# Turning the expert tiles on VectorE in 32x32 blocks, in a two-block decoder kernel

## The reference, cut to what matters

```python
def peer_ffn(h, w_q, sub_keys, expert_u, expert_v):       # 8 heads, 128 x 128 = 16384 experts, top 16
    q = (xb @ w_q).reshape(PEER_BLOCK, PEER_HEADS, 2, PEER_HALF)
    s = jnp.einsum('thjd,hjkd->thjk', q, sub_keys).astype(jnp.float32)
    sv, si = lax.top_k(s, PEER_TOPK)
    cand = sv[:, :, 0, :, None] + sv[:, :, 1, None, :]
    cs, ci = lax.top_k(cand.reshape(PEER_BLOCK, PEER_HEADS, PEER_TOPK * PEER_TOPK), PEER_TOPK)
    ...
    eidx = i1 * PEER_N_KEYS + i2
    g = jax.nn.softmax(cs, axis=-1)
    act = jax.nn.gelu(jnp.einsum('td,thkd->thk', xb, expert_u[eidx]), approximate=False)
    return jnp.einsum('thk,thkd->td', (g * act).astype(v.dtype), expert_v[eidx])
```

## Time and profile before

| | us |
|---|---|
| median of 3 runs | 5112.97 |
| lowest, highest | 5112.11, 5113.0 |
| the profiled execution | 5112.5 |
| its span | 5110.8 |

### The profile page before, as it was taken

One profiled execution on the slowest core, in us unless ns is written; L12 is line 12 of the kernel. 1 busy time (PEld: TensorE's weight loads), 2 busy tenths in 40 slices (PEclk: granted clock), 3 DMA queues, 4 the chain that ended last, 5 costly groups with the idle time before them and its releaser, 6 DMA issues. The chain is left out here.

```text
span 5110.8 us, 60896 instructions
## 1 busy us (share of the span) xinstructions
PE 4680.5 (92%) x23260; PEld 3922.2 (77%) x23260; DVE 2321.4 (45%) x3698; ACT 1421.5 (28%) x1441; POOL 355.4 (7%) x213
## 2 busy tenths in 40 slices
PE   8998998998996879978887799899999999999997
PEld 6886667887885668867777687678888888888886
DVE  4323234324324543224666433356665764455554
ACT  3222432213212332223333212232223333222222
POOL 0000000000000000001111000000000000233331
PEclk9998999999997689978999899999999999999999
DMA  3232012232231022221111222223333444555553
GB/s 107 96 93 70 30 41 74 96 96 87 88 101 42 0 66 93 90 57 58 50 49 41 62 75 94 76 72 125 127 126 128 156 185 168 195 195 195 191 189 114
DMA packets 446288, 511.43 MB, mean 100 GB/s; under 512 B 22104, under 2 KB 394964, under 8 KB 445156
## 3 DMA queue, kind: packets, MB, share of 16 engines
q1 hardware_dynamic: 446180, 510.01, 29.9%
HBM read 440.74 MB, written 69.21 MB: 100 GB/s over the span
## 5 line engine op out<-in xcount | busy, mean ns | idle before, releaser
L78 DVE TENSOR_TENSOR w_lo<-w_raw,w_hi 128x2048 fp32r<-128x2048 f32 (+2 forms) x322 | 672.0, 2089 | 1291.4 <-ACT w_hi L72 1291.4
L72 ACT CAST w_hi<-w_raw 128x2048 fp32r<-128x2048 f32 (+2 forms) x322 | 555.5, 1729 | 1130.6 <-PE psum L2738 491.6
L95 PE MATMUL psum<-h_lo_ffn,w_hi 128*128 128x512 f32 x1280 | 498.2, 389 | 0.0
L96 PE MATMUL psum<-h_hi_ffn,w_lo 128*128 128x512 f32 x1280 | 498.2, 389 | 0.0
L94 PE MATMUL psum<-h_hi_ffn,w_hi 128*128 128x512 f32 x1280 | 498.2, 389 | 0.0
L94 PE MATMUL psum<-h_hi_peer,w_hi 128*128 128x512 f32 x1120 | 445.3, 398 | 3.1 <-DVE w_lo L78 1.9
L96 PE MATMUL psum<-h_hi_peer,w_lo 128*128 128x512 f32 x1120 | 437.3, 390 | 0.0
L95 PE MATMUL psum<-h_lo_peer,w_hi 128*128 128x512 f32 x1120 | 436.4, 390 | 0.0
L2738 PE MATMUL psum<-pr_act_hi,w_lo 128*128 128x512 f32 x1024 | 398.6, 389 | 0.0
L2736 PE MATMUL psum<-pr_act_hi,w_hi 128*128 128x512 f32 x1024 | 398.6, 389 | 0.0
L2737 PE MATMUL psum<-pr_act_lo,w_hi 128*128 128x512 f32 x1024 | 398.6, 389 | 0.0
(11 more groups left out here) (441 smaller groups left out, 8333.1 us busy)
## 6 DMA issues: line engine op xcount, KB each, us to landing
w_raw<-in_ffn_w_gate_up_dram SPq DMA_DIRECT2D x176, 512.0 KB, 4.2
w_raw<-in_peer_u_dram SPq DMA_DIRECT2D x128, 512.0 KB, 4.1
w_raw<-in_peer_v_dram SPq DMA_DIRECT2D x128, 512.0 KB, 4.3
w_raw<-in_w_in_dram SPq DMA_DIRECT2D x64, 512.0 KB, 4.4
peer_hidden<-pr_q SPq DMA_DIRECT2D x64, 512.0 KB, 2.6
peer_gates<-pr_staged SPq DMA_DIRECT2D x8, 4096.0 KB, 12.7
pr_back<-peer_hidden SPq DMA_DIRECT2D x64, 512.0 KB, 6.2
pr_gate<-peer_gates SPq DMA_DIRECT2D x64, 512.0 KB, 7.2
```

The costliest lines, as they stand in the source:

```text
L72: c.nc.scalar.copy(c.hi[:, slot, :cols], c.raw[:, slot, :cols]).then_inc(c.hi_ready, 1)
L78: c.nc.vector.tensor_tensor(c.lo[:, slot, :cols], c.raw[:, slot, :cols], c.hi[:, slot, :cols].bitcast(F32), ALU.subtract).then_inc(c.lo_re ...
L95: c.nc.tensor.matmul(out, w_hi, x_lo, start=False, stop=False)
L96: mm = c.nc.tensor.matmul(out, w_lo, x_hi, start=False, stop=(n == last))
```

## The change

- `turn` moves from TensorE to VectorE: one block transpose of the raw tile in place, each 32x32 block by itself. For that a U tile is loaded in another arrangement, in four DMAs of 32 partitions each with runs of 1 KB. After the turn, partition 32b + j holds features 256b + 32k + j in chunk k, an order of features that differs from that of h. So h is stored in DRAM after the first query tiles and loaded back in that order, chunk by chunk as the last query (now with the chunk as outer loop) frees them.
- hi and lo of a U tile are made from SBUF in two halves, `by_chunk` and `turned_part`.
- `hide` uses banks 0 and 1 or 2 and 3 in turn, and may start before the gelu of the unit ahead.
- Order in a spreading unit: VectorE builds the middle quads of unit x, turns tile n+1, builds the first quads of unit x+1, makes lo of n+1. ScalarE copies hi of n+1 first, then stages all quads.
- `second` of a quad is made by one tensor_tensor instead of four instructions.
- In the norms of width 512 (eight of them) the sum of a token lands in a [128, 4] tile, the root and the reciprocal work on that, and the factor is spread over the identity and summed by a second matmul with ones, which leaves it in PSUM.
- The top-8 steps raise one semaphore at their end instead of one an instruction.

```diff
@@ Norm.vector, Norm.tensor
+        if self.by_token:
+            nc.vector.tensor_scalar(self.col[:, :], self.ps[:, 0, 0:TC], 1.0 / D, EPS, ALU.mult, ALU.add
+                                    ).then_inc(self.steps, 1)
+            dve.wait_ge(self.rooted, run + 1)
+            nc.vector.reciprocal(self.col[:, :], self.col[:, :]).then_inc(self.steps, 1)
...
+            nc.vector.tensor_tensor(rstd[:, :].rearrange("p (t k) -> p t k", t=TC),
+                                    self.c.ident[:, :].unsqueeze(1).broadcast_to(tokens),
+                                    self.col[:, :].unsqueeze(2).broadcast_to(tokens), ALU.mult
+                                    ).then_inc(self.spread, 1)
...
+            for t in range(TC):
+                ins = mm(self.ps[:, 0, t:t + 1], self.sq[:, 0, t * P:(t + 1) * P], self.c.ones[:, 0:1], start=True,
+                         stop=True)
+            ins.then_inc(self.summed, 1)
+            pe.wait_ge(self.spread, self.run + 1)
+            mm(self.ps[:, 0, :], self.c.ones[:, :], self.rstd[:, :], start=True, stop=True).then_inc(self.widened, 1)
@@ SyncE
             def u_tile(use, j, n):
-                load_tile(c, sp, use, j, u_parts(c, j, u, n * 2))
+                sp.wait_ge(c.begun, 1)
+                sp.wait_ge(c.lo_ready, 2 * use + j + 1)
+                rows = u.rearrange("(q e) d -> e q d", e=BAND)
+                for b in range(P // BAND):
+                    dst = c.raw[b * BAND:(b + 1) * BAND, j, :].rearrange("p (q n) -> p q n", n=BAND * KD)
+                    src = rows[:, bass.ds(n * 8, 8), b * BAND * KD:(b + 1) * BAND * KD]
+                    sp.dma_start(dst, src).then_inc(c.tile_loaded[j], 16)
+            def store_h():
+                sp.wait_ge(pre.lo_done, (pre.run + 1) * KD)
+                for m in range(2):
+                    for k in range(KD):
+                        odd, r = k // 4, k % 4
+                        src = h[m][r * BAND:(r + 1) * BAND, odd:KD:2, :].bitcast(F32)
+                        sp.dma_start(h_rows[m, k].rearrange("(b j) t -> j b t", j=BAND), src).then_inc(h_stored, 16)
+            def reload_h():
+                sp.wait_ge(h_stored, ROWS_LOADED + 16 * 2 * KD)
+                for k in range(KD):
+                    sp.wait_ge(h_free, k + 1)
+                    for m in range(2):
+                        sp.dma_start(h[m][:, k, :].bitcast(F32), h_rows[m, k]
+                                     ).then_inc(h_back[k // 4], 16)
...
-            for n in range(3):
-                u_tile(uA + n // 2, n % 2, n)
+            u_tile(uA, 0, 0)
+            u_tile(uA, 1, 1)
+            reload_h()
+            u_tile(uA + 1, 0, 2)
@@ ScalarE
+            def copy_hi(j):
+                for a in range(2):
+                    ins = nc.scalar.copy(by_chunk(c.hi, j, a), turned_part(c, j, a))
+                ins.then_inc(c.hi_ready, 1)
...
                 for x in range(ROUND_UNITS):
                     before, between = quads_of(x)
+                    j = (x + 1) % 2
+                    act.wait_ge(turned, o * ROUND_UNITS + (SPREAD_AT + x + 2))
+                    copy_hi(j)
                     stage(o, before)
-                    act.wait_ge(turned, o * ROUND_UNITS + (SPREAD_AT + x + 2))
-                    act.wait_ge(c.tile_used, o * ROUND_UNITS + (2 * uA + SPREAD_AT + x + 2))
-                    nc.scalar.copy(c.hi[:, (x + 1) % 2, :], turn_ps).then_inc(c.hi_ready, 1)
                     stage(o, between)
@@ VectorE
+            def turn(n):
+                j = n % 2
+                dve.wait_ge(c.tile_loaded[j], 32 * uA + 64 * (n // 2) + 64)
+                dve.wait_ge(c.tile_used, 2 * uA + n + 1)
+                V.transpose(c.raw[:, j, :], c.raw[:, j, :]).then_inc(turned, 1)
...
+                    V.tensor_tensor(second[:, k % RING], c.iota[:, :].unsqueeze(1).broadcast_to(wide),
+                                    chosen[:, 1, toks].unsqueeze(2).broadcast_to(wide), ALU.is_equal)
...
             for n in range(CHOSEN_AT):
-                turned_lo(n)
+                turn(n + 1)
                 piece(EARLY + n)
+                turned_lo(n + 1)
...
+            build(0, quads_of(0)[0])
             for o in range(SPREAD_ROUNDS):
                 for x in range(ROUND_UNITS):
-                    before, between = quads_of(x)
-                    build(o, before)
-                    build(o, between)
-                    turned_lo(SPREAD_AT + o * ROUND_UNITS + x + 1)
+                    n = SPREAD_AT + o * ROUND_UNITS + x + 1
+                    build(o, quads_of(x)[1])
+                    turn(n)
+                    if x + 1 < ROUND_UNITS:
+                        build(o, quads_of(x + 1)[0])
+                    elif o + 1 < SPREAD_ROUNDS:
+                        build(o + 1, quads_of(0)[0])
+                    turned_lo(n)
@@ TensorE
-            pe.sem_inc(gelued, 1)
+            pe.sem_inc(gelued, 2)
...
+            hide(uA, 0, 0, h_is_back)
+            hide(uA, 1, 1)
+            with pe.Fori(1, CHOSEN_AT // 2) as i:
-                turn(uA + i, 1)
                 hide(uA + i, 0, i * 2)
-                turn(uA + i + 1, 0)
                 hide(uA + i, 1, i * 2 + 1)
...
                     spread_quads(o, before)
-                    turn(follow, (x + 1) % 2)
                     wait_tile(c, pe, use, x % 2)
```

More of the change, by code:

```diff
@@ L350, in tensor @@
         pe.wait_ge(self.steps, self.run * self.STEPS + 4)
[L351 to L354, removed]
+        mm = self.c.nc.tensor.matmul
+        if self.by_token:
+            for t in range(TC):
[4 more added lines that the diff above has]
+            mm(self.ps[:, 0, :], self.c.ones[:, :], self.rstd[:, :], start=True, stop=True).then_inc(self.widened, 1)
+        else:
+            for b, (lo, hi) in enumerate(self.banks):
+                ins = mm(self.ps[:, b, :], self.c.ones[:, :], self.sq[:, 0, lo:hi], start=True, stop=True)
+            ins.then_inc(self.summed, 1)
+            pe.sem_inc(self.spread, 1)
+            pe.sem_inc(self.widened, 1)
 def norm(c, tag, gain, h, src=None, width=T, out_f32=None):
@@ L2250, in quads_of, with groups_ended_in, peer @@
     return range(at, at + a), range(at + a, at + a + b)
-def peer(c, gain, w_q, sub_keys, u, v, h, hidden, gates):
+def groups_ended_in(x):
+    before, between = quads_of(x)
+    begin, end = before.start, between.stop
+    return [g for g in range(ROUND_GROUPS) if begin < (g + 1) * GROUP_QUADS <= end]
+def peer(c, gain, w_q, sub_keys, u, v, h, hidden, gates, h_rows):
     nc = c.nc
@@ L2347, in _ @@
                 sp.sem_inc(written[j], 16)
-            with sp.Fori(1, NH // 2) as i:
+            for i in range(1, NH // 2):
                 for j in range(2):
@@ L2655, in queries @@
                 n = i * 2 + j
+                last = isinstance(i, int) and i == NH // 2 - 1 and j == 1
                 if not (isinstance(i, int) and i == 0):
@@ L2658, in queries @@
                     pe.wait_ge(q_taken, n - 1)
+                if last:
+                    jobs = wide_jobs(c, h, j)
+                    for k in range(KD):
+                        for out, pair, _ in jobs:
+                            (w_hi, w_lo), (x_hi, x_lo) = pair(k)
+                            nc.tensor.matmul(out, w_hi, x_hi, start=k == 0, stop=False)
+                            nc.tensor.matmul(out, w_hi, x_lo, start=False, stop=False)
+                            mm = nc.tensor.matmul(out, w_lo, x_hi, start=False, stop=k == KD - 1)
+                        mm.then_inc(h_free, 1)
+                    pe.sem_inc(c.tile_used, 1)
+                elif not (isinstance(i, int) and i == 0):
                     w_hi, w_lo = w_tile(c, j, KD, 256)
@@ L2752, in _ @@
             scores(0, 0)
-            with pe.Fori(1, NH // 2) as i:
+            with pe.Fori(1, NH // 2 - 1) as i:
                 queries(i, 0)
```

167 lines of the change are left out of this document (93 added, 74 removed).

## The result

The changed kernel takes 5069.6 us (median of 12 runs, 5067.7 to 5096.5) against 5111.4 us (12 runs, 5110.6 to 5113.0): a ratio of 0.9938, 95% interval 0.992 to 0.9955. Its runs form two groups with nothing between them: seven at 5067.7 to 5069.9 and five at 5094.8 to 5096.5. The kernel before has one group. The profiled execution is one of the lower group: 5068.3 us, span 5066.6.

The account below looks back on a forecast made before the run. TensorE's list of work bounds the expert layer's long stages. Gains of 2 + 43.2 + 8.9 + 5 less losses of 1 + 38.7 + 1.5 make 17.9 us: 5112.5 to 5095 us, range 5040 to 5150.

Parts of the forecast that it names:

- The turn's price: VectorE's transpose of a 128x2048 tile takes 2.21 us; rival, a slow turn, 5192 us at 4.4 us, chance 0.12.
- the forecast's 2.65: Turn time in us on VectorE at which the whole gain is gone, at 44 us lost per microsecond above 2.21.
- First stage: Units 0 to 33 of the expert layer: 58.4 us from turns off TensorE, less 15.2 given back, 43.2 gained.
- the third kind just fits: First stage: VectorE's turn, lo and third-costliest piece take 10.67 us, within TensorE's 10.89 us a unit.
- the fifth kind: First stage: the fifth kind of VectorE piece is as short as the fourth, which fits easily at 8.35 us.
- Spreading: 24 units of the expert layer: three take 57.65 us against 52.81, so 38.7 us lost, plus 1.5 in the first.
- The stop of 7.4 us: Every third spreading unit: TensorE waits 7.4 us before its third quad on ScalarE's staging, plus 2.0 us of clock.
- The start and the last units: Expert layer's start: 2 us gained by the first hide, 1 lost to stores; last six units: 8.9 us gained.
- The norms: Eight norms of width 512: 6.2 us against 6.9, 0.6 to 0.7 each, 5 us gained, between 0 and 12.
- The loads: U tile loads take about 5 us and fit, nothing charged; rival, they set the pace, 5139 us, chance 0.10.
- The forecast's own range: Whole kernel: 5070 to 5118 us around 5095, for clock loss, norm and seam; the forecast's chance 0.60.
- the rival of the one-operand rate: VectorE's turn runs 1.1 us faster, at the rate of a one-operand op: 5067 us, chance 0.10.

Follow-up runs that it names:

- both kernels that stage first: Changed kernel with ScalarE staging the first quads before waiting for the turn: 5012.5 us; the same plus VectorE turning ahead of the middle quads: ratio 0.9786.
- swapping two calls: Changed kernel with ScalarE staging the first quads before it waits for the turn and copies hi: 5012.5 us, ratio 0.9804.

## Why the forecast was right, and where it was off

**The turn's price.** Taken as 2.21 us, start to next start, from the two-operand op on the same tile. It is 2.24 (3488.25 to 3490.49, where the next instruction starts), and 2.30 from start to end. (The gain would be gone at 2.62 us, 17.9 / 44 above 2.21, and not at the forecast's 2.65.) The Trainium skill, VectorE: DVE Perf Modes, "The three transpose paths", would have made it 5.0 us by its price for a 32x32-block transpose of a 128x128 bf16 tile. The measurement decides: one fp32 instruction over the sixteen tiles of a unit takes 2.30 us, less than half, and the rule to turn on TensorE would have missed what the first stage gains.

**First stage.** 38.7 us gained, 43.2 forecast. The step that was off is the pace of a unit as the longer of the two engines' lists: five units, one head's worth of pieces, should take 12.28 + 11.80 + 3 x 10.89 = 56.75 us, and take 57.8. The transposes show it:

```profile
3488.25 2.31 DVE L2687 STREAM_TRANSPOSE w_raw<-w_raw 128x2048 f32<-128x2048 f32 x1 [0.74 <-PE psum L96]
...
3499.95 2.30 DVE L2687 STREAM_TRANSPOSE w_raw<-w_raw 128x2048 f32<-128x2048 f32 x1
...
3511.46 2.31 DVE L2687 STREAM_TRANSPOSE w_raw<-w_raw 128x2048 f32<-128x2048 f32 x1 [3.70 <-PE psum L96]
...
3522.34 2.31 DVE L2687 STREAM_TRANSPOSE w_raw<-w_raw 128x2048 f32<-128x2048 f32 x1 [2.56 <-PE psum L96]
...
3534.53 2.30 DVE L2687 STREAM_TRANSPOSE w_raw<-w_raw 128x2048 f32<-128x2048 f32 x1
...
3546.02 2.31 DVE L2687 STREAM_TRANSPOSE w_raw<-w_raw 128x2048 f32<-128x2048 f32 x1 [0.73 <-PE psum L96]
```

The steps are 11.70, 11.51, 10.88, 12.19 and 11.49 us. A turn without a wait in brackets was paced by VectorE. The unit behind it is released by TensorE and yet takes 11.51 or 11.49, not 10.88: its turn had started as lo ended, 0.2 us ahead of the first matmul of hide (3500.17), where in a unit paced by TensorE it starts 0.3 us behind it (3511.46 beside 3511.19), and the next turn waits for the end of that hide. Twice a head a hand-over of 0.6 us is paid that the maximum of the two lists doesn't hold; "the third kind just fits" failed by this, and the fifth kind, which had time to spare, pays it too.

**Spreading.** 42.2 us lost, 40.2 forecast; from the first to the last spread quad 461.7 us, some 458 forecast. The stop of 7.4 us is there eight times as worked out. The other waits on the staging are 65.0 - 8 x 7.36 = 6.1 us, one of 1.9 in the first unit and 0.3 in the others, where the forecast had 0.35 a unit and 1.5 for the first one. The stage without stops takes 386.5 us (both kernels that stage first), so of the 84.2 us above that 65.0 are waits and 19 come with them. The stretch at half clock is 6.8 us long, twice that behind the 3.1 us stop of before, but it begins within the stop. TensorE is busy for 32 us in the eight stretches, so by an estimate 16 of the 19 us are clock, 2.0 a stop, as I took; the other 3 are not traced to anything.

**The start and the last units** came as forecast within a microsecond or two (2.3 gained against 1 and a norm's 0.6; 10.4 against 8.9).

**The norms.** Off by a factor of about two: 1.3 us for the one norm read from the trace against 0.6 to 0.7. What eight are worth in the whole kernel is less sure: 12 us by taking them out of the changed kernel, 5 to 7 when put alone into the one before, and 2 for seven of them. The bounds of 0 to 12 hold all of these.

**The loads** are no bound. U tiles now come in 256 KB pieces:

```profile
w_raw<-in_peer_u_dram SPq DMA_DIRECT2D x256, 256.0 KB, 4.7
```

Four of them overlap in a slot, a whole tile takes 7.3 us from its first issue to its last landing (median), more than the "about 5" that I took, and no turn waits for one: in the first stage each turn starts on TensorE's release or right behind the lo part. The Trainium skill, SBUF — State Buffer, "Door 1: The DMA port swizzle", gave 5.5 us by its 189 GB/s, an estimate (that rate is measured at 1 MiB, so the fixed part, which the prediction would add, is in it already); the measured 7.3 us is longer, still fits, and doesn't show whether half of the ports was the limit.

**What was missed.** 29 us in a stage that the diff doesn't touch. The sum had only the stages in which an operation changes; the norms were costed by their own length, not by what they do to the clock in the stages behind them. The forecast's own range, 5070 to 5118, holds the five upper runs and just misses the seven lower ones. Those lie where the rival of the one-operand rate put the time (5067), but the turn took 2.24 us, not 1.1 less, so that is chance. In five of twelve runs the kernel took 5095 to 5096 us, the forecast's number; but with errors of 4.5 us (first stage) and 2 (spreading) on one side and 1.5 (last units), 1 (start) and about 2 (norms) on the other, this is closer than the working deserves.

## What to carry to other kernels

Before moving an operation to an idle engine, write out that engine's order for one period and ask of each wait in it what is queued behind it and who needs that: here one staging behind one wait gave back 42 of the 51 us that taking the turns off TensorE had gained in the other stages, and swapping two calls brought 82 us. When two engines pace units in turn, their lists' maximum is too short by a hand-over at each change. A loop in which TensorE often pauses may run in two patterns of granted clock, and a change in front of it may decide which; compare kernels by groups of runs and by stage, not by medians over both.

## What the runs showed of the hardware

- VectorE turned a 128x2048 fp32 tile in place, in 32x32 blocks, in 2.30 us, as long as a two-operand op of that size (2.29, rows 5).
- The same 520 matmuls of the attention took 120.1 us at a mean clock of 0.68 or 94.2 us at 0.83. The runs of five kernels fall into two groups, 25 to 29 us apart.
- In thirteen profiles the short pattern stands where, and only where, the clock had come back 24.50 to 24.53 us behind the attention's first matmul; at 24.47 us it was the long one.
- A stop of TensorE of 7.4 us cost 2.4 us on top of itself (19.2 / 8), some 2.0 of it by the clock behind it; one of 3.3 us cost 1.3 us ((423.2 - 386.5 - 26.3) / 8).
